# Attention loop of a streaming encoder layer: logits pairs behind the parts, an earlier first output part, and one FFN step moved

## What is computed

```python
x = x + 0.5 * swiglu(rmsnorm(x, ffn1_norm), ffn1_w_gate, ffn1_w_up, ffn1_w_down)
h = rmsnorm(x, mix_norm)
gb, gc, xv, q, k, v, qi, ki, wi = jnp.split(h @ w_in, SPLIT_POINTS, axis=-1)
u = gc * xv                                   # gated convolution, 512 columns
conv = sum(up[:, j:j + T] * conv_w[j] for j in range(CONV_W))
conv_out = gb * conv
...
score = jnp.einsum('bths,bth->bts', jax.nn.relu(dots), wi)    # indexer
_, sel = lax.top_k(score, n_sel)                              # 128 keys (prompt)
logits = jnp.einsum('btkgd,btnkd->btkgn', qg, k_sel) * (HEAD_DIM ** -0.5)
p = jax.nn.softmax(logits, axis=-1)
o = jnp.einsum('btkgn,btnkd->btkgd', p, v_sel)
...
x = x + jnp.concatenate([conv_out, attn], axis=-1) @ w_out
x = x + 0.5 * swiglu(rmsnorm(x, ffn2_norm), ffn2_w_gate, ffn2_w_up, ffn2_w_down)
```

## Time and profile before

| | us |
|---|---|
| median of 3 runs | 1164.75 |
| lowest, highest | 1164.25, 1165.76 |
| profiled execution | 1166.49 |
| its span, first to last instruction | 1164.6 |
| PE busy in the span | 1154.6 |
| DVE, ACT, POOL busy | 916.1, 526.1, 94.7 |
| mean granted clock of PE | 0.994 |

### The profile page before, as it was taken

How to read it: one execution, slowest core, us unless ns; L and a number is a source line. 1 busy time by engine, 2 the same in 40 slices (tenths; PEclk the granted TensorE clock), 3 DMA queues, 4 the chain that set the end, 5 groups by cost and what they waited for, 6 DMA issues and landing times.

```text
span 1164.6 us, 20299 instructions
## 1 busy us (share of the span) xinstructions
PE 1154.6 (99%) x7704; PEld 1107.3 (95%) x7704; DVE 916.1 (79%) x1402; ACT 526.1 (45%) x791; POOL 94.7 (8%) x130
## 2 busy tenths in 40 slices
PE   9999999999999999999999899999999999999999
PEld 9999999999999999867987679999999999999998
DVE  6998777877989982467998753798877778798996
ACT  6354444444445552361234452434444444454452
POOL 0000000000000000102473351000000000000000
PEclk9999999999999999999999899999999999999999
DMA  7212221222332233201321023321322222124222
GB/s 249 85 55 91 86 95 72 98 82 67 124 146 80 73 109 119 73 37 37 145 73 37 1 67 107 129 73 37 109 72 84 96 72 98 64 100 154 103 87 84
DMA packets 22992, 103.98 MB, mean 89 GB/s; under 512 B 3344, under 2 KB 6288, under 8 KB 13584
## 3 DMA queue, kind: packets, MB, share of 16 engines
q1 hardware_dynamic: 21792, 99.67, 24.2%
q10 hardware_dynamic: 1136, 3.43, 1.0%
HBM read 96.99 MB, written 6.10 MB: 89 GB/s over the span
## 4 chain that ended last, share of the span: by engine, by line
PE 91%; DVE 7%; issue 1%; ACT 1%; DVEq 0%; POOL 0%; ACTq 0%; POOLq 0%
PE ps L656 18%; PE ps L658 18%; PE ps L657 18%; PE ps L596 8%; PE ps L600 8%; PE ps L598 8%; PE ps L587 2%; PE ps L589 2%; PE ps L588 2%; DVE score L2063 1%; PE ps L854 1%; DVE top L2062 1%; DVE wl L1548 1%; PE ps L937 1%; PE ps L863 1%
## 5 line engine op out<-in xcount | busy, mean ns | idle before, releaser
L1102 ACT ACTIVATE wh<-raw 128x1024 fp32r<-128x1024 f32 (+4 forms) x206 | 202.4, 985 | 261.6 <-PE ps L658 142.9
L656 PE MATMUL ps<-xs,wh 128*128 128x320 f32 x976 | 300.2, 308 | 0.5 <-ACT snap L1102 0.5
L657 PE MATMUL ps<-xs,wh 128*128 128x320 f32 x976 | 300.2, 308 | 0.0
L658 PE MATMUL ps<-xs,wl 128*128 128x320 f32 x976 | 300.1, 308 | 0.0
L656 PEld LDWEIGHTS ps<-xs,wh 128*128 128x128 f32 x976 | 182.9, 187 | 1.0 <-issue 1.0
L658 PEld LDWEIGHTS ps<-xs,wl 128*128 128x128 f32 x976 | 182.9, 187 | 0.0
L657 PEld LDWEIGHTS ps<-xs,wh 128*128 128x128 f32 x976 | 182.9, 187 | 0.0
L596 PE MATMUL ps<-xh,wh 128*128 128x320 f32 x544 | 131.1, 322 | 0.0
L1672 DVE TENSOR_TENSOR wl<-raw,wh 128x1024 fp32r<-128x1024 f32 (+1 forms) x108 | 112.7, 1044 | 19.4 <-ACT wh L1102 18.3
L600 PE MATMUL ps<-xh,wl 128*128 128x320 f32 x544 | 124.7, 311 | 0.0
L598 PE MATMUL ps<-xl,wh 128*128 128x320 f32 x544 | 124.6, 311 | 0.0
(11 more groups left out here) (282 smaller groups left out, 2134.4 us busy)
## 6 DMA issues: line engine op xcount, KB each, us to landing
raw<-gu SPq DMA_DIRECT2D x42, 1024.0 KB, 4.8
raw<-dn SPq DMA_DIRECT2D x16, 1024.0 KB, 5.3
raw<-dn SPq DMA_DIRECT2D x12, 512.0 KB, 3.8
raw<-wconv SPq DMA_DIRECT2D x6, 1024.0 KB, 4.9
raw<-wout SPq DMA_DIRECT2D x4, 1024.0 KB, 4.8
x<-xt SPq DMA_DIRECT2D x12, 320.0 KB, 4.7
raw<-wtok SPq DMA_DIRECT2D x4, 840.0 KB, 4.3
x_keep<-x SPq DMA_DIRECT2D x8, 320.0 KB, 2.2
```

The costliest lines, as they stand in the source:

```text
L656: pe.matmul(out, ah, bh, start=first, stop=False, skip_group_check=True)
L657: pe.matmul(out, ah, bl, start=False, stop=False, skip_group_check=True)
L658: return pe.matmul(out, al, bh, start=False, stop=last, skip_group_check=True)
L1102: return nc.scalar.activation(out, in_, ACT.Copy, scale=scale)
```

## The change

It has four edits.

1. **Logits pairs.** `issued_by(n)` from item 15 on is n + 4 (it was 19 at item 15 and n + 5 behind it). From item 15 on PE does the logits behind the item's parts, ahead of them before, and DVE does `masked_min` at the end of the item, behind rounds, `proj_out` and quarter. Pair (k, k+1) so moves from the head of item k-4 to the end of item k-3, an odd item; (18, 19) stays in item 15.
2. **Parts.** `parts_by` counts one more from item 8 on: part 32 is issued in item 8 (none was), each later part up to one item earlier, and four parts instead of five stand behind the loop. The convolution chunks are split in items 7 to 10 instead of 8 to 11. Chunk 0 would overwrite what job 11 still reads, so a new semaphore, `chunks_used`, is raised when job 11 has done its fourth part, at the end of item 6, and ScalarE waits for that instead of for the whole job.
3. **Output weights.** U_OUT is split in quarters in items 4 to 7 instead of at once in item 3. The quarters of U_OUT+1 stay in items 14 to 17 (in item 15 ScalarE does its own ahead of the exponentials); those of U_OUT+2 move one item earlier with the jobs.
4. **FFN.** `plain_hid(3)` moves on DVE from ahead of the last pair of sets to the last set (slot 1 of the last pair), ahead of its first `out_of`. ScalarE waits for it ahead of `rest_hi(1)`, a new wait.

```diff
-            return 32 + n - 8 - sum(m <= n for m in WITHOUT_PART)
+            return 32 + n - 7 - sum(m <= n for m in WITHOUT_PART)
...
-        PROJ_SPLITS = {0: U_CONV + 5, item_of(9): U_OUT}
-        QUARTERS = {14 + q: (U_OUT + 1, q) for q in range(4)}
+        PROJ_SPLITS = {0: U_CONV + 5}
+        QUARTERS = {4 + q: (U_OUT, q) for q in range(4)}
+        QUARTERS |= {14 + q: (U_OUT + 1, q) for q in range(4)}
...
-            return min(n + 3 if n < 15 else 19 if n == 15 else n + 5, len(ITEMS))
+            return min(n + 3 if n < 15 else n + 4, len(ITEMS))
...
-        CONV_SPLITS = {8: (0,), 9: (1,), 10: (2,), 11: (3,)}
+        CONV_SPLITS = {7: (0,), 8: (1,), 9: (2,), 10: (3,)}
...
+                if b == NPROJ - 1 and c == 3:
+                    mm.then_inc(chunks_used, 1)
...
-                for ahead in range(issued_by(n - 1), issued_by(n)):
-                    logits(ahead)
+                if n < 15:
+                    for ahead in range(issued_by(n - 1), issued_by(n)):
+                        logits(ahead)
                 for i in range(parts_by(n - 1), parts_by(n)):
                     filler(i)
+                if n >= 15:
+                    for ahead in range(issued_by(n - 1), issued_by(n)):
+                        logits(ahead)
...
+                act.wait_ge(hid_ready, PLAIN * (k + 1))
                 for n in (1, 2):
                     rest_hi(n)
...
-                    act.wait_ge(proj_job, NPROJ)
+                    act.wait_ge(chunks_used, 1)
...
+                    if not ahead:
+                        plain_hid(3)
                     out_of(p, slot, 0, block)
...
-                plain_hid(3)
                 period(PAIRS - 1, 0, pair_block(PAIRS - 1))
...
-                for ahead in range(issued_by(n - 1), issued_by(n)):
-                    masked_min(ahead)
+                if n < 15:
+                    for ahead in range(issued_by(n - 1), issued_by(n)):
+                        masked_min(ahead)
                 for t, rounds in ROUNDS.items():
                     top_rounds(t, rounds.get(n, 0))
...
+                if n >= 15:
+                    for ahead in range(issued_by(n - 1), issued_by(n)):
+                        masked_min(ahead)
```

More of the change, by code:

```diff
@@ L230, in trunk @@
         proj_job = sem("proj_job")
+        chunks_used = sem("chunks_used")
         proj_evac = sem("proj_evac")
@@ L350, in quarters_before @@
         def quarters_before(U):
-            return 3 * (0 if U == U_CONV else U - U_OUT)
+            return 3 * (0 if U == U_CONV else 1 + U - U_OUT)
         def first_part(buf, i):
@@ L894, in proj_part @@
                     pe.wait_ge(lo_ready, U + 1)
-                    if U in (U_CONV, U_OUT + 1, U_OUT + 2):
+                    if U in (U_CONV, U_OUT, U_OUT + 1, U_OUT + 2):
                         pe.wait_ge(quarter_lo, quarters_before(U) + 3)
@@ L1521, in _ @@
                     attended_hi(n // 8 - 1)
-                if n in QUARTERS and ITEMS[n][0] != 4:
+                if n in QUARTERS and (ITEMS[n][0] != 4 or n == 15):
                     quarter_hi_of(*QUARTERS[n])
@@ L1525, in _ @@
                     exp_out(ahead)
-                if n in QUARTERS and ITEMS[n][0] == 4:
+                if n in QUARTERS and ITEMS[n][0] == 4 and n != 15:
                     quarter_hi_of(*QUARTERS[n])
```

## The result

| | before | changed |
|---|---|---|
| median of 6 runs each, us | 1165.20 | 1168.95 |
| lowest, highest | 1164.25, 1166.27 | 1168.31, 1170.77 |
| ratio, 95% interval | | 1.0037 [1.0027, 1.0048] |
| profiled execution | 1166.49 | 1168.67 |
| its span | 1164.6 | 1166.8 |

What follows compares the result with a forecast made beforehand. PE, busy 1154.6 of 1164.6 us, bounds the kernel, leaving its waits and clock. Terms -4.0 (item 8 inside) + 0.6 - 0.8 = -4.2 us give 1160.6 or 1162.3 by reference; the middle, 1161.5, was taken, range 1158.9 to 1164.6.

Steps and rivals of the forecast that it cites:

- FFN, -0.8: In both FFNs: moving plain_hid(3) behind the last gate ends PE's wait for the snapshot; -0.8 us in all.
- Item 8, -0.6: Items 8 and 9: the part moved earlier lies over PE's waits of 0.35 and 0.26 us, which go; -0.6 us.
- Item 15, a wait of about 2.4 where 2.39 was: Item 15: PE's long wait for masked_min is not removed but stands one part later; 0 for this step.
- Items 15 to 22, a gain of 4.0: Up to the start of item 22: 4.0 us gained, between 2.0 and 4.9, mostly half clock not paid; includes item 8's 0.6.
- The slow stretch was short: Attention loop, from item 15's wait on: the clock falls again, but for less than the trace's 13.7 us.
- the second wait: Pair (20, 21): a new 1.8 us wait for masked_min(19), gone if the low clock brings PE there behind DVE.
- From item 21 on there is nothing for PE to wait for.: Later attention items: PE has no waits left there, said against a slower result; no size of its own.
- The last turn, +0.6: End of the loop: pair (38, 39) stands later, its chain needs 3.4 to 3.5 us; +0.6 us, between 0 and 1.2.
- The reference point: Whole kernel: counting from median 1164.75 gives 1160.6, from the profiled 1166.49 gives 1162.3; undecided, middle 1161.5 taken.
- The rival "slower": Attention loop: waits of 2.4 and 1.8 us hold the clock low to past 683; time 1167, chance 0.07.

Runs made afterwards that it cites:

- edit 4 alone: The kernel before with only the FFN edit (plain_hid(3) in the last set): 1162.88 us where before is 1164.00, ratio 0.9992.
- edit 1 undone: The changed kernel with the logits pairs and masked_min back in the old order: 1161.88 us where before is 1164.00, ratio 0.9981.
- edit 1 alone: The kernel before with only logits pairs behind the parts and masked_min at the item's end, from item 15: 1167.88 us where before is 1164.00, ratio 1.0036.

## Why the prediction was wrong, point by point

- **FFN, -0.8.** Right: the snapshot's waits are gone, and alone the edit gives 0.9992, -0.9 us, though the interval just reaches no change.
- **Item 8, -0.6.** The mechanism was right, the term not: it was cancelled. I laid the parts over waits of 0.35 and 0.26 us and said that GpSimd is "done with chunk 0 long before". It is done with chunk 0, but it works on the next ones, and DVE's `conv_lo` beside it takes 2.19 us in item 7 and 1.59 in item 8, instead of 0.81. Turn 9 waits 0.81 for the `normalise` behind the second. With `normalise` ahead of it, turn 9 comes 3.18 us behind turn 8: 2.83 and a part of 1.07 are 3.90, so 0.7 are gained, as forecast.
- **Item 15, a wait of about 2.4 where 2.39 was.** Right: 2.31, behind the part and not ahead of it. My layout put `masked_min(17)` at 660.4 and the pair at 661.1; they stand at 660.64 and 661.34. That the times agree to 0.2 us is partly luck: I had left the FFN edit out of this layout, and had no wait at turn 9; PE was 0.8 early at turn 8 (635.31 against 636.10), and turn 9 took 0.8 back. I counted a quarter ahead of `masked_min(17)` there at its 0.61 us of work; behind item 15 the same step costs what it waits for.
- **Items 15 to 22, a gain of 4.0.** This term was wrong in size and in sign. Counted as I had counted it (the start of turn 22, and a part done more), the two profiled executions give 680.27 - 679.23 + 1.07 = 2.1. That comes from the low clock in the one of the kernel before: the same loop with a slow stretch of 3.4 us (edit 4 alone) takes 41.09 us from turn 8 to turn 22, and against it the changed kernel loses 1.8.
  The slow stretch was short, as forecast, and stretches without a wait of PE inside do come out short: 3.4 us here, with edit 1 undone and with edit 4 alone, against 13.7 with the wait of 1.14 inside. But the second wait was not swallowed (it came behind the stretch, 1.26), and the old order can have a stretch just as short: I took for a gain of the change what lay between two executions. That this sign came true is in part luck. And there were two waits at the turns, 1.67 and 0.67, which I did not have: chain 1. The layout followed DVE and PE only. ScalarE stood in it as a source of exponentials, and not as an engine whose own order has the copy of the weights behind them.
- **"From item 21 on there is nothing for PE to wait for."** This is the step that failed most: 4.5 us between turn 22 and the last turn. I had reasoned that pairs stand two items ahead of their turn; that bounds the chain to the turn, and not the wait of the pair for its bank. Chain 2 has a period of its own, 2.2 to 2.7 us for one item, where PE needs 3.0 for two (turns at 685.42 and 688.45).
- **The last turn, +0.6.** The chain was sized right: GpSimd had the last weights 3.43 us behind the pair's start, where I had 3.4 to 3.5. But the turn, 3.49 behind it, did not wait: the product ahead of it had waited 0.48 for ScalarE's copy, which I did not have.
- **The reference point.** I could not tell whether the profiled 1166.49 was the profiler's or a longer slow stretch. It was the stretch: its mean clock is 0.994. Of the 27 executions of the kernel before beside the first group, 19 have 0.998 or more, and the times follow the clock: 1167.15 us at 0.994, 1163.7 in the mean of ten at 0.998, 1163.8 of eight at 0.999, 1162.52 at 1.000. So most executions of the kernel before had far less than 13.7 us at 1.2 GHz, and the gain that I took from the slow stretch had to be against them: by the slope of these runs, 0.55 us for each 0.001, the 0.005 between the two profiled executions are 2.7 us, but between 0.998 and 0.999 it is 0.6. By this estimate the term of 4.0 was over-sized by some 2 us from the clock alone; the traces above say 3.1.
- **The rival "slower".** It had the right place (`masked_min` behind the round, `proj_out` and the quarter) and came nearest in time, 1167 against 1168.95, at a chance of 0.07. That is luck: it had the wrong mechanism. It priced the lateness through a clock that stays low longer, and the low stretch was shorter. A step that stands behind an operation that waits for another engine has its price without the clock.

## What to carry to other kernels

When a step is put behind another on an engine, ask what that other one waits for, and follow the chain round until it comes back to the step: if it does, the loop has a period, and where the period is longer than the bottleneck's item the loss comes in every item. The busy share does not show it; the pair of rows in which two engines wait for each other in turn does. Keep operations that wait for a second engine behind those that release it, and let the engine idle at the head of its item if it has slack: here that was worth 6.8 us against the changed kernel.

A gain that is read from one profiled execution must be held against the other executions first: a slow stretch of 13.7 us in the profile was 3.4 us in the trace of edit 4 alone, and, as an estimate from the mean clocks of 0.998 and 0.999, some 2 to 5 us in most executions.

## What the runs showed of the hardware

- The clock's fall is not tied to the wait alone. Pair (18, 19) waited 3.10 us in the kernel with edit 1 alone, and 2.39 in the one with edit 4 alone, and its matmuls ran at 2.4 GHz (0.92 us for the group); in the kernel before it waited the same 2.39 and ran at 1.2 GHz (1.65); it waited 1.69 in the kernel with `masked_min` ahead of the quarter and ran at 1.2 GHz (1.55):

```profile
661.11 0.92 PE L937 MATMUL ps<-kt,q_all 64*128 64x384 f32 x4 [3.10 <-DVE stat L2119]
```

```profile
660.70 1.55 PE L941 MATMUL ps<-kt,q_all 64*128 64x384 f32 x4 [1.69 <-DVE stat L2125]
```

  Executions of one and the same kernel have mean clocks from 0.994 to 1.000. The four kernels with `masked_min` at the head of DVE's item have 1.000 in every execution; they wait up to 1.64 us at a turn in the same items, but only 0.7 at pair (18, 19). What decides is open. The Trainium skill (TensorE: Matmul & The Clock Gate, Part 1, What's actually happening) says that how many matmuls at the start of a kernel run at the low clock varies from run to run of one kernel. The runs here show the like in the middle of a kernel: one attention loop had 13.7 us at the low clock in one execution and 3.4 in another.
- DVE and GpSimd stretched each other: 0.81 to 2.19 us for one DVE operation, and 1.55 to 1.88 for GpSimd's.
